# Values of the late attention units in a second PSUM bank, and the second branch turned inside the first output projection

## The reference, cut to what matters

```python
h = x * (1 + sc1) + sh1
qa, ka, va, qb, kb, vb, ga, gb = jnp.split(h @ w_in, W_IN_SPLITS, axis=-1)
...
oa, ob, new_state = mixer(qa, ka, va, qb, kb, vb, pos)
merged = (jax.nn.sigmoid(ga) * (oa.reshape(B, S, DSA_OUT) @ w_pa)
          + jax.nn.sigmoid(gb) * (ob.reshape(B, S, MOBA_WIDTH) @ w_pb))
x = _layer_norm(ALPHA * x + g1 * (merged @ w_o), ln1_g, ln1_b)
h2 = x * (1 + sc2) + sh2
up, gt = jnp.split(h2 @ w_up, 2, axis=-1)
f = (jax.nn.silu(gt) * up) @ w_down
x = _layer_norm(ALPHA * x + g2 * f, ln2_g, ln2_b)
```

## Time and profile before

| | |
|---|---|
| median of 3 runs | 527.13 us (526.14 to 529.02) |
| profiled execution | 526.59 us, of which the span is 525.0 us |
| PE busy | 504.2 us, 96% of the span |
| DVE, ACT, POOL busy | 294.5, 223.3, 95.3 us |
| DMA | 115.80 MB, mean 221 GB/s |
| chain that ended last, by engine | PE 76%, DMA 10%, DVE 4%, ACT 3%, SPq 3%, issue 2% |

### The profile page before, as it was taken

How to read it: one execution, slowest core, us unless ns; L and a number is a source line. 1 busy time by engine, 2 the same in 40 slices (tenths; PEclk the granted TensorE clock), 3 DMA queues, 4 the chain that set the end, 5 groups by cost and what they waited for, 6 DMA issues and landing times.

```text
span 525.0 us, 10079 instructions
## 1 busy us (share of the span) xinstructions
PE 504.2 (96%) x3932; PEld 460.6 (88%) x3932; DVE 294.5 (56%) x564; ACT 223.3 (43%) x370; POOL 95.3 (18%) x137
## 2 busy tenths in 40 slices
PE   5899999999999999998899799999999999999997
PEld 3678889888778998987898499998999999999996
DVE  0556677858445453456965876543644445466344
ACT  1434443325435553447435564563444444333312
POOL 2000121126900000000741509631011100000000
PEclk9899999999999999998999999999999999999999
DMA  7999997496996820842645716599777754364102
GB/s 253 395 393 392 381 392 267 141 381 198 323 330 197 271 82 12 249 147 80 248 154 161 241 51 195 163 376 311 285 258 259 260 166 172 130 210 161 41 0 91
DMA packets 85437, 115.80 MB, mean 221 GB/s; under 512 B 3785, under 2 KB 67465, under 8 KB 84884
## 3 DMA queue, kind: packets, MB, share of 16 engines
q1 hardware_dynamic: 83572, 102.76, 57.7%
q0 software_dynamic: 1824, 12.47, 6.5%
HBM read 111.94 MB, written 13.57 MB: 239 GB/s over the span
## 4 chain that ended last, share of the span: by engine, by line
PE 76%; DMA 10%; DVE 4%; ACT 3%; SPq 3%; issue 2%; POOL 0%; ACTq 0%; DVEq 0%; POOLq 0%
PE psum L750 20%; PE psum L752 19%; PE psum L751 19%; DMA raw<-in_w_in 4%; DMA raw<-in_w_up 3%; PE psum L923 2%; PE psum L1043 2%; DMA x_tok<-in_x_sample 2%; PE psum L996 1%; ACT w_hi L494 1%; PE psum L771 1%; PE psum L1029 1%; PE psum L987 1%; PE psum L782 1%; DVE w_lo L499 1%
## 5 line engine op out<-in xcount | busy, mean ns | idle before, releaser
L750 PE MATMUL psum<-act_hi,w_hi 128*128 128x288 f32 x736 | 221.8, 301 | 8.1 <-DVE act_lo L1856 3.3
L499 DVE TENSOR_TENSOR w_lo<-raw,w_hi 128x1024 fp32r<-128x1024 f32 (+1 forms) x120 | 146.9, 1229 | 145.0 <-ACT w_hi L494 144.8
L751 PE MATMUL psum<-act_lo,w_hi 128*128 128x288 f32 x736 | 217.1, 295 | 0.0
L752 PE MATMUL psum<-act_hi,w_lo 128*128 128x288 f32 x736 | 216.6, 294 | 0.0
L494 ACT ACTIVATE w_hi<-raw 128x1024 fp32r<-128x1024 f32 (+1 forms) x120 | 124.1, 1041 | 104.2 <-PE psum L752 84.7
L750 PEld LDWEIGHTS psum<-act_hi,w_hi 128*128 128x128 f32 x736 | 138.0, 188 | 21.4 <-issue 12.5
L752 PEld LDWEIGHTS psum<-act_hi,w_lo 128*128 128x128 f32 x736 | 138.6, 188 | 0.0
L751 PEld LDWEIGHTS psum<-act_lo,w_hi 128*128 128x128 f32 x736 | 138.3, 188 | 0.1
L750 PE MATMUL psum<-f_hi,w_hi 128*128 128x288 f32 x176 | 52.3, 297 | 0.0
L751 PE MATMUL psum<-f_lo,w_hi 128*128 128x288 f32 x176 | 51.9, 295 | 0.0
L752 PE MATMUL psum<-f_hi,w_lo 128*128 128x288 f32 x176 | 51.8, 294 | 0.0
(11 more groups left out here) (213 smaller groups left out, 590.4 us busy)
## 6 DMA issues: line engine op xcount, KB each, us to landing
ada_s<-in_w_ada SPq DMA_DIRECT2D x22, 1024.0 KB, 10.1
raw<-in_w_up SPq DMA_DIRECT2D x22, 1024.0 KB, 5.4
raw<-in_w_in SPq DMA_DIRECT2D x17, 1024.0 KB, 9.8
raw<-in_w_down SPq DMA_DIRECT2D x10, 1024.0 KB, 5.1
out<-in_cache_kv_a POOLq DMA_DIRECT2D x16, 504.0 KB, 7.0
raw<-in_w_o SPq DMA_DIRECT2D x4, 1024.0 KB, 6.2
raw<-in_w_in SPq DMA_DIRECT2D x4, 768.0 KB, 11.1
kvin<-in_cache_kv_a SPq DMA_DIRECT2D x8, 256.0 KB, 3.5
```

The lines of the kernel that those rows point to most:

```text
L499: nc.vector.tensor_tensor(part(w_lo, slot4, by_rows), raw_half(rslot, hh, by_rows), part(w_hi, slot4, by_rows).bitcast(F32), ALU.subtract) ...
L750: nc.tensor.matmul(out, hi_l, hi_r, start=start, stop=False, skip_group_check=True)
L751: nc.tensor.matmul(out, hi_l, lo_r, start=False, stop=False, skip_group_check=True)
L752: return nc.tensor.matmul(out, lo_l, hi_r, start=False, stop=stop, skip_group_check=True)
```

## The change

Four edits:

1. `values_bank(u)`: units 5, 7, 9 and 11 put their values product into bank 5, the others stay in bank 6. From unit 6 on `prompt_values(u)` waits for `o_ready` u - 1 where it waited for u.
2. ACT's list: branch A's leading part and that of the sample tokens come ahead of the first sigmoids, and `oT_leading(1)` ahead of the sigmoids of blocks 28 to 31.
3. PE's list: `outputs_turn(1)` goes from ahead of quarter 0 to between its second and third output block.
4. DVE's list: `out_copy(10)` goes behind `oT_rest(0)`, and `out_copy(11)` behind the rest of the sample tokens.

```diff
+def values_bank(u):
+
+    return 5 if u >= 5 and u % 2 else 6
...
             if u >= 1:
-                pe.wait_ge(o_ready, u)
+                pe.wait_ge(o_ready, u if u < 6 else u - 1)
...
-                        mm = nc.tensor.matmul(psum[:, 6, E * i:E * i + E], prbT[:, u % 2, 128 * n:128 * n + 128],
+                        mm = nc.tensor.matmul(psum[:, values_bank(u), E * i:E * i + E], prbT[:, u % 2, 128 * n:128 * n + 128],
...
-        pe.wait_ge(o_ready, N_UNITS)
-        outputs_turn(1)
-
-
         for h in range(4):
...
                 mm.then_inc(half_used if m == 3 else pab_done, 1)
+                if n == 1:
+                    pe.wait_ge(o_ready, N_UNITS)
+                    outputs_turn(1)
...
-        act.wait_ge(acc_free[0], 18)
-        act.wait_ge(acc_free[1], 18)
-        sigmoids(22, 24)
-
         def oT_leading(br):
...
                              ACT.Copy).then_inc(oT_h, 1)
+        act.wait_ge(acc_free[0], 18)
+        act.wait_ge(acc_free[1], 18)
+        sigmoids(22, 24)
+        oT_leading(1)
         sigmoids(28, 32)
-        oT_leading(1)
...
-                ins = V.tensor_scalar(o_tokens[:, t, br, E * h:E * h + E], psum[:, 6, E * i:E * i + E],
+                ins = V.tensor_scalar(o_tokens[:, t, br, E * h:E * h + E], psum[:, values_bank(u), E * i:E * i + E],
...
-            if s >= 4:
+            if 4 <= s < 14:
                 out_copy(s - 4)
...
         oT_rest(0)
+        out_copy(N_UNITS - 2)
         dve.wait_ge(oT_h, 2)
...
+        out_copy(N_UNITS - 1)
         oT_rest(1)
```

## The result

| | before | changed |
|---|---|---|
| median | 527.55 us | 529.89 us |
| runs | 22 (525.58 to 533.83) | 22 (526.10 to 535.09) |
| profiled execution | 526.59 us, span 525.0 | 529.87 us, span 528.2 |

The ratio of the changed kernel to the one before is 1.004 with a 95% interval of 1.0021 to 1.006: slower by some 2.1 us (1.1 to 3.2). The medians are over all runs, while the ratio leaves out those over 1.5% above the fastest of their kernel (534.30 and 535.09 us of the changed one). I had forecast 527.6 us with 529.5 as the upper end. The positions of the chain came as worked out, to within 0.15 us; what they were compared with was wrong.

What follows compares the result with a forecast made beforehand. PE was taken to bound the kernel, busy 504.2 of 525.0 us. Quarter 2 starting 0.5 us late, added to the median of 527.13, gave 527.6 us; own range 526.4 to 528.4, eight in ten 525.9 to 529.5.

Steps and rivals of the forecast that it cites:

- The wait of unit 11 and the start of quarter 0: PE: the 1.08 us values wait goes, mostly returning ahead of quarter 0, which starts at 241.2 instead of 242.17.
- The chain behind branch B's turn: ACT, then DVE: split, sigmoids and weight split follow the turn's end at 243.5; PE's quarter 2 starts at 250.6.
- the 0.4 us more: ACT's table load: with the page's drain, first sigmoids would end at 243.9 and the sum be 0.4 us higher.
- I therefore carry the sum to the start of quarter 2: PE: quarter 2's start decides the later chain; 250.6 against 250.10 before, so 0.5 us late.
- ACT had 1.2 us of slack there: ACT, between last sigmoid and `w_hi`: moving branch B's turn uses up the 1.2 us, so the sigmoids are late next.
- I take full clock for the changed kernel: PE around quarter 0: no slow stretch, since PE would stand some 0.9 us instead of 1.35 before it.
- Rival A: PE's clock still drops at 242.05: 1.0 us later, 528.6 us; 0.8 more if all 12 matmuls are slow; chance 0.22.
- Rival B: New waits before quarters 1 and 2 slow PE's clock in quarters 2 and 3: 529.1 to 529.6 us; chance 0.12.
- Rival C: Sigmoids do not bind because splits or calls overlap more; PE keeps its gains, 525.2 us; chance 0.09.
- rival D: No visible effect: wait gone, wait come back, 527.1 us; its chance is counted within the forecast's 0.57.
- The level: The kernel before's median, 527.13 us, to which the forecast added 0.5 us.

Runs made afterwards that it cites:

- e1: The kernel before, unchanged, run and profiled again; ratio to before 1.001 (0.9983 to 1.0037).
- e4: Changed kernel with ACT's weight split of quarter 0's slot moved ahead of the last two sigmoid calls; ratio to before 1.0011 (0.9979 to 1.0043).
- e3: Changed kernel with branch B's turn put back ahead of quarter 0; ratio to before 1.0038 (1.0004 to 1.0072).
- e6: Changed kernel with the sigmoid call over blocks 28 to 31 back ahead of branch B's split; ratio to before 1.0021 (0.9991 to 1.0051).
- e7: Changed kernel with both the edit of e4 and that of e6; ratio to before 1.0011 (0.9977 to 1.0044).
- e8: The same kernel as e4, profiled again; one execution, 533.86 us.
- e2: Kernel before with edit 1 alone (second values bank, looser wait); ratio to before 1.0004 (0.998 to 1.0029).
- e5: The changed kernel, unchanged, run and profiled again; ratio to before 1.0037 (1.0013 to 1.0061).

## Why the prediction was wrong, point by point

- **The wait of unit 11 and the start of quarter 0: right.** I had the wait gone and quarter 0 at 241.2, that is 2.95 after branch A's turn, behind a wait of 0.9. It is 2.85, behind 0.76.
- **The chain behind branch B's turn: right.** The turn's end at 5.25 was to be followed by quarter 2 at 12.35; it was 5.12 and 12.21. Quarter 1 came at 7.45 as forecast. The waits before quarters 1 and 2 were to be 0.6 and 1.5 to 1.8; they are 0.73 and 1.33, the second a little below its range. The table load is hidden, and the first sigmoid starts 1.29 us after it starts, in both kernels. No drain shows, so the 0.4 us more that I had worked out from the Trainium skill's page "ScalarE: Activation LUTs" (What ACT_TABLE_LOAD costs) did not come.
- **"I therefore carry the sum to the start of quarter 2", 0.5 us late against 250.10: this is the step that failed.** The 250.10 was the start in an execution with 1.5 us of slow clock in quarter 0. I took this stretch as part of the kernel before, priced its end as a gain of the change, and set the changed kernel at full clock against it. e1 has the same waits with the clock at 1.00 and quarter 2 at 10.44, where 250.10 is 11.85. The same sum against 10.44 is 12.35 - 10.44 = 1.9; measured is 1.77. I forecast 0.5.
- **"ACT had 1.2 us of slack there": wrong for the same reason.** In e1 it has none.
- **"I take full clock for the changed kernel", because of the shorter stand: right in both profiles of it, but not for that reason.** e4 has the same instructions up to this point and the same 0.76 wait, and fell to 0.50 in quarter 0. Rival A was thus a matter of the execution, for both kernels alike. With all 12 matmuls slow I had priced it at 1.0 + 0.8 = 1.8 us, where its own terms give 0.64 for the other six and so 1.6; in e4, which had the stretch over them, quarter 1 came 1.54 us late.
- **Rival B did not come.** The clock stays at 1.00 over the new waits before quarters 1 and 2 in both profiles of the changed kernel. My ground against it was weak, though: I had one wait of 1.64 us amid 288-column matmuls that left the clock at 1.00. Two more waits amid 288-column matmuls, for `act_lo`, stand some 58 and 63 us after branch A's turn. The first is 1.54 us in all ten profiles, the second 1.8 us in nine, and in five of the ten the clock fell behind one of them (e3, e4, e6, e7, e8). So that B stayed away in these two profiles may be luck. Rival C did not come either: in the changed kernel the sigmoids bind, as e3, e6 and e8 show. Of rival D the edit 1 part is true: that wait comes back ahead of quarter 0 (e2).
- **The level.** The median of before was 527.13 in 3 runs and 527.55 in 22, 0.4 of the difference. With it, 527.55 + 1.8 = 529.3; the remaining 0.5 or so is inside the interval of the ratio (1.1 to 3.2 us), and no run here assigns it to a place. Nor did the changed kernel merely meet more slow stretches. Most executions on record come with their mean granted clock. A straight line through time against this clock, over 75 executions of the kernel before and 34 of the changed one, taken in several batches, puts the changed kernel 2.2 us (1.6 to 2.8) higher at equal clock; within the batch of e5 alone it is 1.8 (0.9 to 2.8).

The rows of before would have allowed the right comparison: the earlier trace rows showed a stretch at half clock behind a short wait and none behind a longer one, so the waits alone did not explain it, and the sum should have been made against both levels, 250.10 and 248.6, with the second as the reference if such a stretch can fall anywhere. The second gives 250.6 - 248.6 = 2.0, and 527.13 + 2.0 = 529.1 us.

## What to carry to other kernels

A stretch of slow clock in one profile is an event of that execution until a second profile has it at the same place; work out a change against the kernel at full clock, and give the event to both sides. When a wait is filled by starting work earlier, look at what was moved back to make room: here a transpose of 0.6 us, moved back by 1.5 us, and a sigmoid call of 1.06 us, put behind its split, delayed a list of ACT that was already as long as PE's work beside it. An engine's idle time can be slack that another stall has made, and goes when that stall goes.

## What the runs showed of the hardware that I had not expected

Each of the ten profiles has one to four stretches in which PE was granted 1.2 GHz, some 3.4 us each and one of 6.8 (at 368 us in e2), and their places differ between executions of one kernel: 13 and 242 us in the first profile of before and 57 us in e1; 146 us in the first profile of the changed kernel and 57 us in e5; 57 and 368 us in e2; 301 in e3; 240 and 302 in e4; 297 in e6; 301 in e7; 57, 156, 306 and 375 us in e8. They fall on a few places, each in a wait of PE of 0.76 to 2.7 us or within some 5 us behind it. Which of them is hit is not set by the kernel's instructions alone: before and e1, and changed and e5, are pairs of one kernel with no place in common. One in quarter 0 costs 1.4 to 1.5 us (11.85 against 10.44, 8.99 against 7.45). Branch A's turn moves between 237.68 and 242.86 us in the same ten profiles, by these stretches and by waits for DMAs at the start; so single runs differ by several us.
